# The first projections of a three-block transformer on one core: order of loads, of the first weight pieces and of the gate products

## The reference, cut to what matters

```python
def even_mixer(x, w_in, gla_gate_w2, gla_gate_b, ..., w_out):
    p = x @ w_in
    p_gla, p_rw = p[..., :GLA_IN], p[..., GLA_IN:]
    ...
    p_rw = p_rw + rw_mu * (token_shift(p_rw) - p_rw)
    r, k, v, wl, al, gl = jnp.split(p_rw, RW_OFFSETS, axis=-1)
    w = -jax.nn.softplus(-(rw_w0 + jnp.tanh(wl) @ rw_w2)) - 0.5
    decay = jnp.exp(-jnp.exp(w.astype(jnp.float32)))
    a = jax.nn.sigmoid(rw_a0 + al @ rw_a2)
    g = jax.nn.sigmoid(gl) @ rw_g2
    kk = heads(k * rw_k_k, RW_N).astype(jnp.float32)
    kk = kk * lax.rsqrt(jnp.maximum(jnp.sum(kk * kk, -1, keepdims=True), 1e-24))
    k = k * (1 + (a - 1) * rw_k_a)
    ...
```

## Time and profile before

| | us |
|---|---|
| median of 3 runs | 1186.43 |
| lowest and highest | 1185.67, 1188.95 |
| the profiled execution | 1188.14 |
| its span, first to last instruction | 1186.3 |
| mean granted clock of TensorE | 0.951 of full |

### The profile page before, as it was taken

One profiled execution on the slowest core, in us unless ns is written; L12 is line 12 of the kernel. 1 busy time (PEld: TensorE's weight loads), 2 busy tenths in 40 slices (PEclk: granted clock), 3 DMA queues, 4 the chain that ended last, 5 costly groups with the idle time before them and its releaser, 6 DMA issues.

```text
span 1186.3 us, 16936 instructions
## 1 busy us (share of the span) xinstructions
PE 1098.8 (93%) x7036; PEld 970.3 (82%) x7036; DVE 726.3 (61%) x1004; ACT 517.5 (44%) x736; POOL 133.6 (11%) x151
## 2 busy tenths in 40 slices
PE   5998899988999999888889899999979997999998
PEld 4798899866999988676667799998769866999885
DVE  3476875576766575746674676666664556666343
ACT  3453242244444443424663444343255656555331
POOL 1004663114000000510000400000110000000000
PEclk9897899989899999888999899999989999999999
DMA  9332002124887777253783587767534332665540
GB/s 293 106 121 75 1 1 72 63 85 137 297 275 224 252 271 278 71 180 132 115 209 107 177 282 256 253 236 281 184 106 143 107 93 85 184 191 196 189 166 36
DMA packets 113581, 193.67 MB, mean 163 GB/s; under 512 B 4674, under 2 KB 85073, under 8 KB 113378
## 3 DMA queue, kind: packets, MB, share of 16 engines
q1 hardware_dynamic: 109842, 179.66, 45.2%
q0 software_dynamic: 3248, 11.83, 4.5%
q10 hardware_dynamic: 416, 1.11, 0.2%
HBM read 188.39 MB, written 4.19 MB: 162 GB/s over the span
## 4 chain that ended last, share of the span: by engine, by line
PE 82%; DVE 8%; ACT 5%; issue 2%; SPq 1%; DMA 1%; POOL 1%; DVEq 0%; ACTq 0%; POOLq 0%
PE ps L415 22%; PE ps L417 22%; PE ps L416 22%; PE ps L1971 2%; PE ps L1956 2%; PE ps L1185 2%; PE ps L1949 1%; PE ps L1195 1%; PE ps L1422 1%; PE ps L1129 1%; DVE ARR L399 1%; DVE XL L551 1%; ACT ARR L386 1%; PE ps L481 1%; DMA ring<-in_ffn_w_gate_up_dram 1%
## 5 line engine op out<-in xcount | busy, mean ns | idle before, releaser
L399 DVE TENSOR_TENSOR ARR<-ring,ARR 128x2048 fp32r<-128x2048 f32 (+1 forms) x143 | 321.2, 2251 | 209.7 <-ACT ARR L386 209.7
L415 PE MATMUL ps<-XH,ARR 128*128 128x256 f32 x1232 | 354.6, 288 | 15.4 <-DVE XL L551 8.7
L386 ACT ACTIVATE ARR<-ring 128x2048 fp32r<-128x2048 f32 (+1 forms) x143 | 267.0, 1874 | 204.8 <-PE ps L417 149.6
L416 PE MATMUL ps<-XL,ARR 128*128 128x256 f32 x1232 | 351.6, 285 | 0.0
L417 PE MATMUL ps<-XH,ARR 128*128 128x256 f32 x1232 | 351.4, 285 | 0.0
L415 PEld LDWEIGHTS ps<-XH,ARR 128*128 128x128 f32 x1232 | 238.1, 193 | 20.7 <-issue 16.9
L416 PEld LDWEIGHTS ps<-XL,ARR 128*128 128x128 f32 x1232 | 238.1, 193 | 0.1
L417 PEld LDWEIGHTS ps<-XH,ARR 128*128 128x128 f32 x1232 | 238.0, 193 | 0.0
L415 PE MATMUL ps<-ARR 128*128 128x512 f32 x420 | 171.0, 407 | 8.9 <-DVE ARR L503 4.6
L416 PE MATMUL ps<-ARR 128*128 128x512 f32 x420 | 167.5, 399 | 0.0
L417 PE MATMUL ps<-ARR 128*128 128x512 f32 x420 | 167.4, 399 | 0.0
(11 more groups left out here) (343 smaller groups left out, 1278.9 us busy)
## 6 DMA issues: line engine op xcount, KB each, us to landing
ring<-in_ffn_w_gate_up_dram SPq DMA_DIRECT2D x44, 1024.0 KB, 5.9
ring<-in_w_dram SPq DMA_DIRECT2D x32, 1024.0 KB, 5.2
ring<-in_w_ada_dram SPq DMA_DIRECT2D x24, 1024.0 KB, 5.3
ring<-in_ffn_w_down_dram SPq DMA_DIRECT2D x22, 1024.0 KB, 5.0
ring<-in_even_w_in_dram SPq DMA_DIRECT2D x13, 1024.0 KB, 5.6
ring<-in_w_in_dram SPq DMA_DIRECT2D x9, 1024.0 KB, 5.3
ring<-in_mla_w_q_b_dram SPq DMA_DIRECT2D x6, 768.0 KB, 6.7
ring<-in_even_w_out_dram SPq DMA_DIRECT2D x4, 1024.0 KB, 4.8
```

Source lines behind the costliest of these rows:

```text
L386: e.activation(split(i)[0], raw(i), ACT.Copy).then_inc(*up("hi", ("hi", i)))
L399: e.tensor_tensor(lo, raw(i), hi.bitcast(F32), ALU.subtract).then_inc(*up("lo", ("lo", i), ("raw free", i)))
L415: e.matmul(out, lhs[0], rhs[0], start=first, stop=False)
L416: e.matmul(out, lhs[0], rhs[1], start=False, stop=False)
```

## The change

1. `x` is loaded in two halves of rows: the top one is SP's first load, the low one is ACT's second, behind the identity.
2. The half piece rw14 comes ahead of rw12 in the list of pieces, so it is multiplied first.
3. rw12 is split by its two blocks of columns on ACT and on DVE, and PE waits for each block by itself (`one_by_one`).
4. The transposes of `VR` stand behind rw14 and rw12 on PE. The `memset` of a column of `PT` stands first on DVE.
5. The splits of rw12 and rw4 stand further ahead on DVE, and that of rw6 between the shifts of rw14 and rw12.
6. The block of gates is cut: decay stays behind rw6, rates and squares stand behind rw0, the output gate behind rw8; ACT and DVE follow.
7. On SP the fourth piece (rw6) stands ahead of the small matrices and of `CST`, and the three broadcast rows come behind the sixth piece, under a semaphore of their own.

```diff
-        plan_columns("rw12", WIN, 8, RW_COLS[12:])
+        plan_columns("rw14", WIN, 8, RW_COLS[14:])
+        plan_columns("rw12", WIN, 8, RW_COLS[12:14])
...
+        def act_split_columns(e, i):
+            done["hi"] = i + 1
+            e.wait_ge(*at(("raw", i)))
+            for h in range(2):
+                o = slice(h * P, h * P + P)
+                e.activation(split(i)[0][:, :, o], raw(i)[:, :, o], ACT.Copy).then_inc(*up("hi", ("hi", i, h)))
+
+        def dve_split_columns(e, i):
+            done["lo"] = i + 1
+            hi, lo = split(i)
+            for h in range(2):
+                o = slice(h * P, h * P + P)
+                e.wait_ge(*at(("hi", i, h)))
+                e.tensor_tensor(lo[:, :, o], raw(i)[:, :, o], hi[:, :, o].bitcast(F32), ALU.subtract).then_inc(
+                    *up("lo", ("lo", i, h), *([("raw free", i)] if h else [])))
...
         def sp_start(e):
+            e.dma_start(X[:, 0, :], a["x"][0, 0:P, :]).then_inc(*up("x_top", "x top", by=16))
             for i in range(NRAW):
                 sp_piece(e, i)
...
+            sp_piece(e, NRAW)
+            e.dma_start(W2A2[0:64, :], a["rwkv_w2"][0]).then_inc(*up("even", by=16))
...
             e.dma_start(CST[:, P:], a["consts"][:, P:WIDE - P]).then_inc(*up("consts", by=16))
...
+            sp_piece(e, NRAW + 1)
+            sp_piece(e, NRAW + 2)
+            e.dma_start(LNG, a["rwkv_ln_g"].to_broadcast([P, 512])).then_inc(*up("even_out", by=16))
...
         def act_start(e):
-            e.dma_start(X, a["x"].rearrange("b (t p) d -> p (b t) d", p=P)).then_inc(*up("x", "x", by=16))
             e.dma_start(CST[:, 0:P], a["consts"][:, 0:P]).then_inc(*up("ident", "ident", by=16))
+            e.dma_start(X[:, 1, :], a["x"][0, P:2 * P, :]).then_inc(*up("x_low", "x low", by=16))
             act_split(e, weights[0])
             act_halves(e, "x0", XT, 8, [])
+            act_split_columns(e, weights[1])
...
         def tensor(e):
             pe_start(e)
-            pe_shift(e, 12, 3)
+            pe_shift(e, 14, 1)
+            pe_shift(e, 12, 2, one_by_one=True)
+            pe_vectors(e)
             pe_shift(e, 4, 4)
-            pe_gates(e)
-            pe_shift(e, 0, 4)
+            pe_decay_gate(e)
+            pe_shift(e, 0, 2)
+            pe_rates(e)
+            pe_shift(e, 0, 4, 2)
             pe_decay(e)
-            pe_shift(e, 8, 4)
+            pe_shift(e, 8, 2)
+            pe_output_gate(e)
+            pe_shift(e, 8, 4, 2)
...
         def scalar(e):
...
-            act_shift(e, 12, 3)
+            act_shift(e, 14, 1)
+            act_shift(e, 12, 2)
+            act_shift(e, 4, 2)
             act_low_rank(e)
-            act_shift(e, 4, 4)
-            act_gates(e)
-            act_shift(e, 0, 4)
+            act_shift(e, 4, 4, 2)
+            act_decay_gate(e)
+            act_shift(e, 0, 2)
+            act_rates(e)
+            act_shift(e, 0, 4, 2)
+            act_lengths(e)
             act_decay(e)
...
```

More of the change, by code:

```diff
@@ L417, in mm3, with pe_columns @@
             return e.matmul(out, lhs[1], rhs[0], start=False, stop=last)
-        def pe_columns(e, tag, n_cols, xT, xready):
-            for i in range(0, n_cols, 2):
+        def pe_columns(e, tag, n_cols, xT, xready, first=0, one_by_one=False):
+            for i in range(first, n_cols, 2):
                 w = place_of[tag, i]
@@ L803, in pe_start, with pe_shift, act_shift @@
                 e.transpose(b[:, 0:128], VR[:, h, :], ident).then_inc(*up("turned", ("full", ("vec", h))))
[L806 to L810, removed]
+        def pe_shift(e, i0, n, first=0, one_by_one=False):
+            pe_columns(e, f"rw{i0}", n, XT, xt_step("x0"), first, one_by_one)
+        def act_shift(e, i0, n, first=0):
+            for i in range(first, n, 2):
                 act_split(e, ahead(f"rw{i0}", i))
@@ L830, in dve_shift_pair, with dve_shift @@
                                        ALU.mult, ALU.add).then_inc(*up("shift", ("p", j)))
-        def dve_shift(e, i0, n, then=None):
-            for i in range(0, n, 2):
+        def dve_shift(e, i0, n, first=0):
+            for i in range(first, n, 2):
                 dve_split(e, ahead(f"rw{i0}", i))
                 dve_shift_pair(e, i0 + i)
-                if then:
-                    then(i // 2)
         def act_low_rank(e):
@@ L864, in pe_gates, with pe_output_gate @@
                          ).then_inc(*up("gates", ("full", ("a", i))))
+            for i in range(0, 4, 2):
+                b = bank(e, ("sq", i))
+                e.wait_ge(*at(("kk", i)))
+                e.matmul(b[:, 0:256], cst("heads"), KP[:, i, :], start=True, stop=True)
+                e.wait_ge(*at(("kk", i + 1)))
+                e.matmul(b[:, 256:512], cst("heads"), KP[:, i + 1, :], start=True, stop=True
+                         ).then_inc(*up("gates", ("full", ("sq", i))))
+        def pe_output_gate(e):
             for t in range(2):
@@ L872, in pe_gates, with act_decay_gate @@
                          ).then_inc(*up("gates", ("full", ("g", t))))
[L873 to L881, removed]
+        def act_decay_gate(e):
             e.wait_ge(*at("columns"))
@@ L887, in act_gates, with act_rates @@
                     *up("low", ("sig", t), ("free", ("sig", t))))
+        def act_rates(e):
             for i in range(4):
@@ L893, in act_gates, with act_lengths, act_output_gate @@
                     *up("low", ("aa", i), ("free", ("a", i))))
+        def act_lengths(e):
+            for i in range(0, 4, 2):
+                e.wait_ge(*at(("squares", i)))
+                e.activation(KP[:, i:i + 2, :], KP[:, i:i + 2, :], ACT.Sqrt).then_inc(*up("low", ("length", i)))
+        def act_output_gate(e):
             for t in range(2):
@@ L896, in act_gates, with dve_keys @@
                 e.activation(G[:, t, :], ps(("g", t)), ACT.Copy).then_inc(*up("low", ("g", t), ("free", ("g", t))))
-            for i in range(0, 4, 2):
-                e.wait_ge(*at(("squares", i)))
-                e.activation(KP[:, i:i + 2, :], KP[:, i:i + 2, :], ACT.Sqrt).then_inc(*up("low", ("length", i)))
-        def dve_gates(e):
+        def dve_keys(e):
             e.wait_ge(*at("columns"))
@@ L1210, in dve_bonus @@
                 e.wait_ge(*at(("vt", 1)))
-                e.wait_ge(*at("even"))
+                e.wait_ge(*at("even out"))
                 e.wait_ge(*at(("g", 1)))
@@ L2552, in vector @@
             dve_start(e)
-            dve_shift(e, 12, 3)
+            dve_shift(e, 14, 1)
+            dve_split(e, weights[3])
+            dve_shift(e, 12, 2)
             dve_shift(e, 4, 4)
-            dve_gates(e)
-            dve_shift(e, 0, 4, lambda i: dve_unit_key(e, i))
-            dve_shift(e, 8, 4, lambda i: dve_unit_key(e, i + 2))
+            dve_keys(e)
+            dve_shift(e, 0, 2)
+            dve_squares(e)
+            dve_shift(e, 0, 4, 2)
+            dve_unit_key(e, 0)
+            dve_unit_key(e, 1)
+            dve_shift(e, 8, 2)
+            dve_unit_key(e, 2)
+            dve_shift(e, 8, 4, 2)
+            dve_unit_key(e, 3)
             dve_split(e, ahead("glr", 0))
@@ L2613, in sync @@
             sp_start(e)
-            for i in range(NRAW, len(pieces)):
+            for i in range(NRAW + 3, len(pieces)):
                 sp_piece(e, i)
```

44 lines of the change are left out of this document (26 added, 18 removed).

## The result

| | us |
|---|---|
| kernel before, median of 4 (lowest, highest) | 1186.51 (1185.67, 1188.95) |
| changed kernel, median of 4 (lowest, highest) | 1177.95 (1176.30, 1179.73) |
| ratio with its 95% interval | 0.9921 [0.9892, 0.9950] |
| span of the profiled execution, before and after | 1186.3, 1177.3 |

The time fell by 8.6 us. The forecast was 11, with 1175.4 in a range of 1171.5 to 1179.8; the range held, and the gain came out a fifth smaller. The span of the trace fell by 9.0.

A forecast was written before the change was run, and what follows sets the result against it. PE, busy 93% of the span, bounds the kernel through its waits and slower clock. 7.05 + 1.7 (full clock in rw4 and rw6) + 3.7 - 1.7 = 10.75, say 11 us: 1186.4 becomes 1175.4, range 1171.5 to 1179.8.

The forecast's parts named there:

- Start: First column matmul, half piece rw14 first: starts at 11.2 us instead of 16.56, 5.4 us earlier.
- x ahead: Loads of x ahead of the weights: PE begins at 6.3 us instead of 8.3, 2.0 earlier, bounds 0.5 to 2.7.
- rival (c): Loads at the start or before rw0: x or rw0 lands late, 8 us of gain, 1178.5 us; chance 0.1.
- rw14 and rw12: First column matmuls on PE: 9.95 us kept as before, slower clock included, ending at 21.15 us.
- Hole before rw4: PE's wait before rw4: goes, so rw4 starts at 21.5 us instead of 28.55, 7.05 earlier in all.
- rw6's early load: SP's queue: rw6 loaded at 14.1 us instead of 19.5, lands at about 20, needed by ACT at 21.3.
- Gates: Gate products behind rw6, spread out: 3.7 us gained at full clock, 1.7 lost behind decay, bounds 0 and 3.4.
- rival (b): Clock in the gates falls as long or oftener: 1.7 to 3.4 us more, 1178 us; chance 0.17.
- Rival (a): Clock never falls after the decay block: gives back 1.7 us, 1173.7 us; chance 0.2.
- Behind it: From the hole before qk on: hole stays as long, qk near 81 us instead of 91.7, gain carried to the end.
- (d): Clock falls elsewhere in the whole run: little arrives, gain 4 us or less; chance 0.05.
- (e): Decay block waits for CST: kernel slower, 1191 us if CST lands at 50; chance 0.02.

The follow-up runs named there:

- e3: Changed kernel with x loaded whole by ACT ahead of the identity, as before; ratio 0.9897 [0.9871, 0.9923].
- e5: Changed kernel with added PE products before and behind the transposes of x; no whole time given, rw4 starts at 19.74 us.
- e4: Changed kernel with rw6's load issued behind the small matrices and CST again; no whole time given, rw4 to decay products 16.5 us instead of 11.5.
- e8: Changed kernel with 8 added PE products in the hole before qk; no whole time given, qk to the transposes of KT and BT 15.94 us.
- e2: Changed kernel with decay products in halves, behind rw6 and behind rw0, and rates behind the output gate; 1177.98 us, ratio 0.9909 [0.9881, 0.9936].
- e7: Changed kernel with rw12 split whole, in one operation on ACT and one on DVE; no whole time given, rw4 starts at 21.28 us.
- e11: Changed kernel with decay products in halves and x loaded whole by ACT as before; 1175.98 us, ratio 0.9898 [0.9867, 0.9930].
- e0: Changed kernel run again without edits; median of six 1179.46 us, ratio 0.9923 [0.9896, 0.9950] to the kernel before.
- e10: Changed kernel with the transposes of VR ahead of the columns on PE again; no whole time given, rw4 starts at 27.40 us.

## Why the prediction was right, and by how much it was off

**Start, right.** 11.2 forecast, 11.14 measured, by the way that was worked out: rw14's load, ACT's split, DVE's split, first quarter of the halves.

**x ahead, right in kind and without worth.** It came 3.0 us earlier and not 2.0. The 2.0 us stand in no term of the sum, but the forecast let rw14 land behind `x`, and rival (c) priced a late `x` at 1 us. e3 shows rw14 there at the same time with `x` as before; a later `x` costs 0.3 at the first column and nothing at rw4.

**rw14 and rw12, a term too small.** I kept the 9.95 us of before, with the slower clock in them; it took 11.05 here, and in e5, with full clock, 8.6. rw4 was 6.2 us early and not 7.05.

**Hole before rw4, right.** It is gone, and rw4 and rw6 take 11.53 us where 11.4 were forecast. rw6's early load, which the forecast named with 1.3 us of slack, carries 5 us (e4).

**Gates, right in kind, a term too small.** Rates, squares and output gate took 3.6 and 3.4 us, 7.0 where 6.9 were forecast. But the fall behind the decay block was taken as 3.4 us of half clock, 1.7 lost, and was 6.8 in this trace: 0.9 in the last decay product and 2.4 in rw0 (48 matmuls in 8.1 us and not 5.7), 3.3 lost. So the whole step brought 0.4 us in this trace (14.9 before, 14.5 now), where 3.7 less 1.7 = 2.0 were forecast; with the mean fall of the nine traces it would be 1.6. The nine traces have 0 once, 3.4 five times and 6.8 three times, 4.2 in the mean, so the size was near the mean and rival (b) is what the first trace shows. Rival (a), no fall, came in one of nine.

**Behind it.** The hole before qk was 4.07 and not 3.67, but the way through it is as long as before: from ACT's copy of rw10 to the first matmul of qk 6.86 us before (84.83 to 91.69) and 6.87 now (76.83 to 83.70). PE only got through the half piece glr 0.4 us sooner behind rw10. qk came 8.0 us early: 10.75 less 1.0 by the start of the decay products, 1.6 by their clock, and 0.15 in the rest. From qk to the keys it then took 15.9 us instead of 17.0, because the slow stretch behind the hole was 3.4 us and not 6.8 and GpSimd's chain came to bind (e8). So the keys are 9.1 early and the span 9.0 shorter. That this stage could give back 1.1 us is a term that the forecast did not have, and it is luck: in e2, e7 and e11 the same stretch was 6.8 us long, and the stage took 16.4 to 17.1.

**Rivals (d) and (e)** did not come: the lead of the keys is the lead of the end to 0.1 us, and `CST` was never waited for in the new place. But so close a match is chance: in e0 the keys are 12.9 us early and the end 10.3, so the lead is not carried whole, as the forecast had it.

**The range.** Its lower end does not follow from the terms given for it: 1175.4 less 0.7 (`x`) and 1.7 (no fall) is 1173.0 and not 1171.5.

## What to carry to other kernels

Waits side by side at a start don't add up: list all that must be there before the first useful matmul, and move the last, then the next, since one left in place takes back everything (`VR` here), and one moved ahead of need brings nothing (`x`). Put the smallest piece of weights first where its buffer is what the third piece waits for. Do not trust a long row of matmuls on few rows to keep the clock, even if PE is never idle in it: try them cut up between full ones, check the clock in several traces, for one shows only one throw, and then check that the time follows, which it did not clearly do here.

## What the runs showed of the hardware that I had not expected

- The granted clock fell with PE busy without a break, in eight of nine traces behind 4.2 us of products on 64 rows and one row, and in none of three when these stood in two blocks of 2.1 us.
- Two traces of one kernel differed by 3.9 us at 80 us into it, mostly by this, and six runs of it by 7.5 us (1174.66 to 1182.16).
- The clock column reads 1.00 before its first recorded change, while eight transposes take 1.97 us there and 1.04 with a busy start.
- The last of the 14 small loads ended PE's wait at 16.44 (e10) and at 16.22 (before), though in e10 it was issued 1.1 us earlier. In e10 the load of rw6 is issued right behind it; whether that holds it up is open.
